# A decoder layer's expert loop: one copy of the down projection behind two copies of gate_up

## The chip, the cores and the metric

The kernel runs on one core of one Trainium2 chip. The metric is the device time of one execution in microseconds (us), lower is better. A core has five engines, each with a sequencer that reads its own stream of instructions: TensorE (PE; weight loads are listed as PEld, the sequencer's own instructions as PEldq), VectorE (DVE), ScalarE (ACT), GpSimd (POOL) and SyncE (SP). Sixteen DMA engines move data, and also instructions, from HBM.

## What is computed

One layer of a decoder: a mixer (retention and stick-breaking attention), then a mixture of experts over 1024 tokens of width 1024, top 4 of 32 experts. What matters here is the expert part:

```python
    def expert_block(args):
        xb, e = args
        gu = xb @ w_gate_up[e] + b_gate_up[e]
        gate = jnp.minimum(gu[:, 0::2], SWIGLU_LIMIT)
        up = jnp.clip(gu[:, 1::2], -SWIGLU_LIMIT, SWIGLU_LIMIT)
        hidden = (up + 1.0) * gate * jax.nn.sigmoid(SWIGLU_ALPHA * gate)
        return hidden @ w_down[e] + b_down[e]
```

The tokens of each expert are gathered, run through this block, weighed with their softmax share and added into the output. The number of tokens of an expert is known only on the chip.

## The kernel before

One block serves one expert with up to 168 tokens (CAP): 128 (P) in the main part and two overflow quarters of 32 (OV) behind them. An expert with more tokens would get further blocks behind the 32 (the second loop, L1165 to L1168). All engines run the blocks in step, tied by semaphores; every engine's order is written out by hand, no planner sets it. The weights of gate_up come in four DMAs of 2 MB and those of down in two, each issued by SP as soon as the block before has used its buffer.

PE's part of a block is block_matmuls (L1111 to L1145). In order: gate_up, for f in 0 to 7 (L1113): 16 fp32 products each (L1119) into bank 0 or 1, with a moving width of `w` tokens; token_list (24 small products for the next block's token list, L1053) behind f = 3; down's bias and its first half (t = 0, L1084 and L1099), each k waiting for the hidden rows that ACT and DVE made (h_lo) and for split weights (c_lo); the second half (t = 1) up to k = 3; turn_tokens, which transposes the next block's tokens (L1060, L1064); k = 4 to 6; the overflow rows' bias (L1090); the overflow rounds, down_over(0) if the block has over 128 tokens and down_over(1) if over 160 (L1107, 32 fp32 products each); and k = 7. An fp32 product of L1119 or L1107 is two MATMULs and two LDWEIGHTS in PE's stream.

The width must be fixed in the code, so there are two copies, WIDTHS = (140, 168). block_pe (L1147) loads the number of tokens into a register and choose (L1150) branches between them: the narrow copy for up to 140 tokens, the wide one for more. Each copy is all of block_matmuls, and the loop over the 32 experts (`with e.Fori(0, NE) as n`, L1163) holds both. In the built program PE's part of this loop is 1,838 instructions; the second loop has as many again. A narrow block runs the header and the narrow copy, then jumps (L1155) over the wide copy to the loop's end, and from there (L1163) back to the top. A wide block jumps over the narrow copy first.

Of the kernel before, what the change touches and what calls it, by code (L numbers as in the profile page):

```python
# [37 lines left out]
P = 128  # L38
# [12 lines left out]
OV = 32  # L51
# [66 lines left out]
def layer(nc, x, attn_norm_g, w_in, ret_norm_g, sb_q_norm_g, sb_k_norm_g, w_out, ffn_norm_g,  # L118
          w_router, b_router, w_gate_up, b_gate_up, w_down, b_down, consts, rope, out):
    with ExitStack() as ctx:  # L120
# [709 lines left out]
        def _(e):  # L830
# [210 lines left out]
            for j in range(NT - 1):  # L1041
                n = NT - 1 - j
# [7 lines left out]
            def token_list():  # L1050
                for h in range(NH):
                    for i in range(NT):
                        mm = e.matmul(bank[7][:, 5 * h:5 * h + 5], hot[:, i, h * P:(h + 1) * P], tw_s[:, i, :],  # L1053
                                      start=i == 0, stop=i == NT - 1)
                mm.then_inc(l_sum, 1)

            def turn_tokens():
                for m in range(2):
                    for q in range(4):
                        mm = e.transpose(bank[4 + m][:, q * P:(q + 1) * P], xg[:, (4 * m + q) * P:(4 * m + q + 1) * P], ident)  # L1060
                    mm.then_inc(g_tr, 1)
                for r in range(RO):
                    for c in range(2):
                        mm = e.transpose(bank[6][:, (2 * r + c) * P:(2 * r + c + 1) * P], xg_o[:, r, c * P:(c + 1) * P], ident)  # L1064
                    mm.then_inc(g_tr, 1)
# [17 lines left out]
            def down_bias(t):  # L1083
                e.matmul(bank[2 + t][:, :], sel, bias_d[:, t * CH:(t + 1) * CH], start=True, stop=False,  # L1084
                         skip_group_check=True)

            def over_bias():
                for r in range(RO):
                    for j in range(GR):
                        e.matmul(bank[7][quarter_rows(j), r * 2 * P:(r + 1) * 2 * P], sel[:, 0:OV],  # L1090
                                 bias_d[:, j * 2 * P:(j + 1) * 2 * P], start=r == 0, stop=False, skip_group_check=True)

            def down_main(n, t, k):
                if t == 0:
                    e.wait_ge(h_lo, n * 8 + (k + 1))
                if k % 2 == 0:
                    e.wait_ge(c_lo, n * 8 + (4 * t + k // 2 + 1))
                for h, w in ((hid_hi, dn_hi), (hid_lo, dn_hi), (hid_hi, dn_lo)):
                    mm = e.matmul(bank[2 + t][:, :], h[:, k], w[:, t, k], start=False, stop=k == KD - 1 and w is dn_lo,  # L1099
                                  skip_group_check=True)  # L1100
                if k == KD - 1:
                    mm.then_inc(m_dn, 1)

            def down_over(r):
                for k in range(KD):
                    for j in range(GR):
                        e.matmul(bank[7][quarter_rows(j), r * 2 * P:(r + 1) * 2 * P],  # L1107
                                 hid[:, k, P + r * OV:P + (r + 1) * OV], dn_ring[:, k, j * 2 * P:(j + 1) * 2 * P],
                                 start=False, stop=k == KD - 1, skip_group_check=True)

            def block_matmuls(n, w, tokens):  # L1111
                e.wait_ge(g_xT, n * 4 + 4)
                for f in range(KD):  # L1113
                    if f % 2 == 0:
                        e.wait_ge(gu_in[f // 2], n * 16 + 16)
                    e.wait_ge(m_up, n * 8 + (f + 1))
                    for part in range(2):
                        for k in range(KD):
                            mm = e.matmul(bank[f % 2][:, part * CAP:part * CAP + w],  # L1119
                                          gu_ring[:, k, f * 256 + part:(f + 1) * 256:2], xT[:, k, 0:w],  # L1120
                                          start=k == 0, stop=k == KD - 1)
                    mm.then_inc(m_gu, 1)
                    if f == 3:
                        e.wait_ge(l_hot, n + 2)
                        e.wait_ge(m_yo, n * 4 + 4)
                        token_list()
                e.wait_ge(s_sel, n + 1)
                down_bias(0)
                for k in range(KD):
                    down_main(n, 0, k)  # L1130
                down_bias(1)
                for k in range(4):
                    down_main(n, 1, k)
                e.wait_ge(g_in, n * 48 + 96)
                turn_tokens()
                for k in range(4, KD - 1):
                    down_main(n, 1, k)
                e.wait_ge(l_ok, n + 2)
                over_bias()
                with e.If(tokens > P):  # L1140
                    down_over(0)
                if w > P + OV:
                    with e.If(tokens > P + OV):
                        down_over(1)
                down_main(n, 1, KD - 1)  # L1145

            def block_pe(n):  # L1147
                tokens = e.value_load(it_i[0:1, 1, bass.ds(n, 1)], min_val=-S, max_val=S)

                def choose(widths):  # L1150
                    if len(widths) == 1:
                        block_matmuls(n, widths[0], tokens)
                        return
                    half = len(widths) // 2
                    with e.If(tokens <= widths[half - 1]):  # L1155
                        choose(widths[:half])
                    with e.Else():
                        choose(widths[half:])

                choose(WIDTHS)  # L1160

            e.wait_ge(it_step, 1)
            with e.Fori(0, NE) as n:  # L1163
                block_pe(n)
            more = e.value_load(it_i[0:1, 1, NI - 1:NI], min_val=0, max_val=NX - 1)  # L1165
            with e.If(more > 0):
                with e.Fori(NE, more + NE) as n:
                    block_pe(n)  # L1168
# [458 lines left out]
```

## Time and profile before

| | us |
|---|---|
| median of 3 runs | 2245.34 |
| lowest, highest | 2244.52, 2245.95 |
| the profiled execution | 2247.83 |
| its span, first to last instruction | 2246.0 |
| PE busy in it | 2148.1 (96%) |
| DVE busy | 1282.2 (57%) |
| ACT busy | 765.2 (34%) |

The profiled execution is 2.49 us above the median of the runs; 1.83 us of it lie outside the span. The mixer takes the first 650 us or so, the expert loop runs from about 670 us to 2229 us. A chain of waits is read from the last instruction backwards: at each step it names the work that the next one waited for. "issue" in it is time in which the engine waited for nothing that the profile shows. [...]

### The profile page before, as it was taken

To read this page: it belongs to the slowest core of one execution; us is meant where nothing else is said; L and a number is where in the kernel's file an instruction comes from. 1 tells how busy PE (TensorE), PEld (TensorE's weight loads), DVE (VectorE), ACT (ScalarE), POOL (GpSimd) and SP (SyncE) were. 2 spreads that over 40 slices of the span, in tenths; PEclk is the share of its full clock that TensorE was granted. 3 is DMA by queue.
4 is the path that set the end of the run, shared out by engine and by line. 5 is a ranking of instruction groups with operands and counts; after the bars stand their busy time and mean duration, and the time that the engine had idled before them with its cause. 6 is when DMAs were issued, how large, how long until landed. Compare 5 with 4: busy or idle time off the path is not lost.

```text
span 2246.0 us, 41668 instructions
## 1 busy us (share of the span) xinstructions
PE 2148.1 (96%) x16349; PEld 1929.3 (86%) x16350; DVE 1282.2 (57%) x2579; ACT 765.2 (34%) x1360; POOL 330.6 (15%) x237
## 2 busy tenths in 40 slices
PE   6999999899969999999999999999999999999996
PEld 5888888677858999899989998999899998999996
DVE  6434534786356565456656654665566665566654
ACT  3243133576113333233333332332333333333332
POOL 1100200200000211112112111111121211212111
PEclk9999999999969999999999999999999999999998
DMA  5231221304365888678979887887798897899983
GB/s 171 79 103 57 94 94 38 113 2 151 113 213 182 287 303 309 221 247 312 324 256 314 310 296 251 289 303 254 268 315 310 309 311 255 283 313 334 331 275 95
DMA packets 257670, 510.12 MB, mean 227 GB/s; under 512 B 7450, under 2 KB 44366, under 8 KB 257294
## 3 DMA queue, kind: packets, MB, share of 16 engines
q1 hardware_dynamic: 234268, 451.96, 56.7%
q0 software_dynamic: 21968, 51.67, 9.4%
q10 hardware_dynamic: 1344, 5.14, 0.7%
q8 instruction: 75, 1.23, 0.2%
q14 instruction: 15, 0.12, 0.0%
HBM read 473.09 MB, written 33.55 MB: 226 GB/s over the span
## 4 chain that ended last, share of the span: by engine, by line
PE 93%; issue 2%; DVE 2%; DMA 1%; POOL 0%; ACT 0%; SPq 0%; ACTq 0%; DVEq 0%; POOLq 0%
PE bank L1119 45%; PE bank L1099 16%; PE bank L860 13%; PE bank L1107 3%; PE bank L958 2%; PE bank L971 2%; PE bank L1005 1%; PE bank L1006 1%; PE bank L1007 1%; PE bank L1060 1%; PE bank L1053 1%; PE bank L942 1%; PE bank L1026 1%; PE bank L1064 1%; PE bank L1084 1%
## 5 line engine op out<-in xcount | busy, mean ns | idle before, releaser
L1119 PE MATMUL bank<-hx,ring 128*128 128x140 f32 (+1 forms) x8192 | 1035.3, 289 | 21.2 <-issue 18.8
L1119 PEld LDWEIGHTS bank<-hx,ring 128*128 128x128 f32 x8192 | 1027.4, 198 | 26.0 <-issue 21.0
L1099 PE MATMUL bank<-work_r,hx_r 128*128 128x512 f32 x1024 | 335.2, 408 | 0.0
L1551 DVE TENSOR_TENSOR mix_r<-ring,work_r 128x1024 fp32r<-128x1024 f32 x256 | 305.1, 1223 | 41.1 <-ACT work_r L792 41.0
L809 ACT ACTIVATE hx<-hx 128x168 f32<-128x168 f32 x256 | 87.9, 344 | 616.1 <-DVE hx L1567 615.0
L1567 DVE TENSOR_SCALAR hx<-bank,small 128x168 f32<-128x168 f32 x256 | 100.4, 392 | 307.7 <-PE bank L1119 307.5
L792 ACT ACTIVATE work_r<-ring 128x1024 fp32r<-128x1024 f32 x256 | 257.7, 1042 | 0.0
L1099 PEld LDWEIGHTS bank<-work_r,hx_r 128*128 128x128 f32 x1024 | 188.2, 189 | 43.8 <-issue 10.4
L1099 PE MATMUL bank<-mix_r,hx_r 128*128 128x512 f32 x512 | 200.0, 391 | 0.0
L800 ACT ACTIVATE hx<-bank,small 128x512 f32<-128x512 f32 x64 | 44.0, 688 | 314.6 <-PE bank L1064 167.9
L603 POOL DMA_INDIRECT out_x<-hx,small x32 | 51.9, 1622 | 658.6 <-ACT hx L802 639.6
L579 POOL DMA_INDIRECT hx<-xn_scratch,small x33 | 33.3, 1009 | 618.7 <-DVE small L1469 618.7
L860 PE MATMUL bank<-hx_r,mix_r 128*128 128x512 f32 x480 | 114.1, 396 | 7.6 <-DVE hx_r L1201 7.6
L815 ACT ACTIVATE hx_r<-hx 128x128 fp32r<-128x128 f32 x256 | 79.0, 308 | 109.7 <-DVE hx L1577 109.7
L860 PEld LDWEIGHTS bank<-hx_r,mix_r 128*128 128x128 f32 x480 | 90.7, 190 | 27.8 <-issue 9.1
L1099 PEld LDWEIGHTS bank<-mix_r,hx_r 128*128 128x128 f32 x512 | 96.1, 188 | 21.0
L860 PE MATMUL bank<-hx_r,work_r 128*128 128x512 f32 x480 | 113.7, 394 | 0.0
L1460 DVE TENSOR_TENSOR work<-hx,cst 128x3072 bf16<-128x3072 f32 x33 | 110.6, 3352 | 0.0
L860 PEld LDWEIGHTS bank<-hx_r,work_r 128*128 128x128 f32 x480 | 89.7, 188 | 20.2 <-issue 1.9
L606 POOL DMA_INDIRECT out_x<-hx,small x64 | 100.4, 1570 | 19.5 <-issue 19.5
L1569 DVE TENSOR_SCALAR hx<-bank,small 128x168 f32<-128x168 f32 x256 | 98.2, 384 | 0.0
L1474 DVE TENSOR_TENSOR hx<-bank,small 128x512 f32<-128x512 f32 x66 | 42.6, 686 | 85.9 <-PE bank L1060 85.9
(220 smaller groups left out, 2335.6 us busy)
## 6 DMA issues: line engine op xcount, KB each, us to landing
ring<-in_w_gate_up SPq DMA_DIRECT2D x128, 2048.0 KB, 12.7
ring<-in_w_down SPq DMA_DIRECT2D x64, 2048.0 KB, 13.8
mix<-in_w_in SPq DMA_DIRECT2D x14, 1024.0 KB, 5.1
work<-in_w_in SPq DMA_DIRECT2D x14, 1024.0 KB, 5.1
ring<-in_x SPq DMA_DIRECT2D x8, 512.0 KB, 8.9
hx<-in_w_out SPq DMA_DIRECT2D x1, 4096.0 KB, 14.7
work<-in_x ACTq DMA_DIRECT2D x8, 512.0 KB, 4.7
out_x<-work SPq DMA_DIRECT2D x8, 512.0 KB, 4.4
```

The lines of the kernel that those rows point to most:

```text
L606: e.indirect_dma_start(out=out_quarters, in_=y_o[:, r], in_offset=None, compute_op=ALU.add, out_offset=bass.IndirectOffsetOnAxis(ap=idx_sc ...
L792: e.activation(dn_hi[:, nh, k:k + 2], dn_ring[:, k:k + 2, nh * CH:(nh + 1) * CH], ACT.Copy).then_inc(c_hi, 1)
L809: e.activation(sg[:, f % 2], g1[:, f % 2], ACT.Sigmoid, scale=GALPHA).then_inc(m_sig, 1)
L815: e.activation(hid_hi[:, f], hid[:, f, 0:P], ACT.Copy).then_inc(h_hi, 1)
L860: mm = e.matmul(dst, lhs, rhs, start=k == 0 and (xs is x_hi and ws is w_hi), stop=k == KD - 1 and ws is w_lo)
L1099: mm = e.matmul(bank[2 + t][:, :], h[:, k], w[:, t, k], start=False, stop=k == KD - 1 and w is dn_lo, skip_group_check=True)
L1107: e.matmul(bank[7][quarter_rows(j), r * 2 * P:(r + 1) * 2 * P], hid[:, k, P + r * OV:P + (r + 1) * OV], dn_ring[:, k, j * 2 * P:(j + 1) * ...
L1119: mm = e.matmul(bank[f % 2][:, part * CAP:part * CAP + w], gu_ring[:, k, f * 256 + part:(f + 1) * 256:2], xT[:, k, 0:w], start=k == 0, sto ...
L1460: e.tensor_tensor(hot, pos_s.unsqueeze(2).to_broadcast([P, NT, NH * P]), slot_at.unsqueeze(1).to_broadcast([P, NT, NH * P]), ALU.is_equal) ...
L1551: e.tensor_tensor(dn_lo[:, nh, k:k + 2], dn_ring[:, k:k + 2, nh * CH:(nh + 1) * CH], dn_hi[:, nh, k:k + 2].bitcast(F32), ALU.subtract).the ...
L1567: e.tensor_scalar(g1[:, b], bank[b][:, 0:CAP], be[:, f:f + 1], GLIM, ALU.add, ALU.min)\
L1569: e.tensor_scalar(u1[:, b], bank[b][:, CAP:2 * CAP], be[:, 8 + f:9 + f], GLIM + 1.0, ALU.add, ALU.min).then_inc(m_up, 1)
```

## The change

block_matmuls is cut in two: gate_up(n, w), which still exists in two widths inside the choice, and down(n, tokens), which stands once behind it. With the second overflow round no longer tied to the wide copy, its test stands inside that of the first.

```diff
-            def block_matmuls(n, w, tokens):
+            def gate_up(n, w):
                 e.wait_ge(g_xT, n * 4 + 4)
                 for f in range(KD):
...
                         token_list()
+
+            def down(n, tokens):
                 e.wait_ge(s_sel, n + 1)
                 down_bias(0)
                 for k in range(KD):
...
                 over_bias()
                 with e.If(tokens > P):
                     down_over(0)
-                if w > P + OV:
                     with e.If(tokens > P + OV):
                         down_over(1)
                 down_main(n, 1, KD - 1)
...
                 def choose(widths):
                     if len(widths) == 1:
-                        block_matmuls(n, widths[0], tokens)
+                        gate_up(n, widths[0])
                         return
...
                 choose(WIDTHS)
+                down(n, tokens)
```

In the built program PE's part of the loop is now 1,569 instructions, again with a second loop like it. The products that a block executes are the same. On PE, at the end of the narrow gate_up, there stood before (each row is an instruction or a run of equal ones; ISA and REGISTER_ALU are the sequencer's register work, names in brackets are semaphores waited for):

```order
L1119 MATMUL bank1<-hx,ring 128x140 x15
L1127 REGISTER_ALU
L1084 MATMUL bank2<-cst,small 128x512 [waits s_sel]
L1099 MATMUL bank2<-work_r,hx_r 128x512 [waits c_lo,h_lo]
L1099 MATMUL bank2<-work_r,hx_r 128x512
```

and now:

```order
L1119 MATMUL bank1<-hx,ring 128x140 x15
L1156 UNCONDITIONAL_BRANCH
...
L1119 MATMUL bank1<-hx,ring 128x168 x15
L1158 UNCONDITIONAL_BRANCH
L1129 REGISTER_ALU
L1084 MATMUL bank2<-cst,small 128x512 [waits s_sel]
L1095 ISA
L1099 MATMUL bank2<-work_r,hx_r 128x512 [waits c_lo,h_lo]
L1099 MATMUL bank2<-work_r,hx_r 128x512
```

A narrow block now jumps (L1156) over the wide gate_up, and a register operation (L1095) stands ahead of each k of down's first half, where the numbers to wait for were kept from gate_up before. L1158 is a jump to the next instruction and isn't in the final stream.

On PE, at the overflow rounds and the end of the loop, there stood before in the wide copy:

```order
L1140 COMPARE_AND_BRANCH
L1107 MATMUL bank7<-ring,hx 32x256 x32
L1140 UNCONDITIONAL_BRANCH
L1143 COMPARE_AND_BRANCH
L1107 MATMUL bank7<-ring,hx 32x256 x32
L1143 UNCONDITIONAL_BRANCH
L1099 MATMUL bank3<-work_r,hx_r 128x512 x2
L1099 MATMUL bank3<-mix_r,hx_r 128x512
L1157 UNCONDITIONAL_BRANCH
L1163 REGISTER_ALU
L1163 COMPARE_AND_BRANCH
```

and now, for both widths:

```order
L1142 COMPARE_AND_BRANCH
L1107 MATMUL bank7<-ring,hx 32x256 x32
L1144 COMPARE_AND_BRANCH
L1107 MATMUL bank7<-ring,hx 32x256 x32
L1144 UNCONDITIONAL_BRANCH
L1099 MATMUL bank3<-work_r,hx_r 128x512 x2
L1099 MATMUL bank3<-mix_r,hx_r 128x512
L1165 REGISTER_ALU
L1165 COMPARE_AND_BRANCH
```

The narrow copy's exit (L1155 before) is gone, and a block with at most 128 tokens jumps over both rounds at once. L1165 is now what L1163 was, the jump back to the loop's top.

## Rows read from the trace of the kernel before

**Rows 1.** The page, chain that ended last by engine.

```profile
PE 93%; issue 2%; DVE 2%; DMA 1%; POOL 0%; ACT 0%; SPq 0%; ACTq 0%; DVEq 0%; POOLq 0%
```

**Rows 2.** PE groups by shape: line, tiles, shapes, count | busy us, mean ns | idle.

```profile
L1119 PE MATMUL bank<-hx,ring 128*128 128x140 f32 x6912 | 847.8, 285 | 18.0 <-issue 15.7 <-DVE hx L1569 1.5 <-DVE hx L1482 0.8
...
L1119 PE MATMUL bank<-hx,ring 128*128 128x168 f32 x1280 | 187.5, 309 | 3.1 <-issue 3.1
```

**Rows 3.** Chain in order of time (start us, us, what): undisturbed halves of gate_up.

```profile
870.94 18.24 PE bank L1119 x128
...
988.48 15.25 PE bank L1119 x128
...
2003.40 15.25 PE bank L1119 x128
...
2047.85 15.26 PE bank L1119 x128
```

**Rows 4.** The same chain: gate_up's end in block 1, and five gaps.

```profile
708.91 0.22 PE bank L1084
...
725.64 3.00 issue
728.64 17.19 PE bank L1119 x128
...
928.31 3.12 issue
931.43 21.39 PE bank L1119 x128
...
1370.89 4.31 issue
1375.20 18.38 PE bank L1119 x128
...
1572.53 4.13 issue
1576.66 18.34 PE bank L1119 x128
...
1907.27 4.29 issue
1911.56 18.15 PE bank L1119 x128
```

**Rows 5.** Stretches: us, busy us (count) of PE, PEld, DVE, ACT, POOL; clock, DMA, GB/s.

```profile
0.00:640.00 640.00, 600.21 (x3841) 502.51 (x3842) 333.53 (x456) 254.43 (x427) 57.55 (x39) 0.99 0.28 92
...
683.58:685.06 1.48, 0.00 (x1) 0.00 (x1) 1.02 (x4) 1.33 (x2) 0.00 (x0) 1.00 0.12 18
...
1375.20:1381.10 5.90, 5.90 (x25) 5.90 (x26) 0.00 (x0) 0.00 (x0) 3.06 (x2) 0.50 1.04 300
```

**Rows 6.** PE's sequencer by line: count, ns min/median/max, first and last start us.

```profile
L1127 PEldq ALU_OP  x1: 32/32/32, 706.6 to 706.6; - x1
...
L1155 PEldq COMPARE_BRANCH  x1: 3547/3547/3547, 723.3 to 723.3; - x1
...
L1163 PEldq COMPARE_BRANCH  x32: 67/209/4897, 727.0 to 2226.5; - x32
```

**Rows 7.** DMA queues (packets, MB, share): 0-640, 660-668, 870-925, 987-1036, 1036-1317 us (last two rows).

```profile
q8 instruction: 31, 0.51, 0.3%
...
q8 instruction: 1, 0.02, 0.9%
...
q8 instruction: 4, 0.07, 0.5%
...
q8 instruction: 3, 0.05, 0.4%
...
q1 hardware_dynamic: 37440, 75.50, 75.0%
q0 software_dynamic: 4032, 9.44, 13.7%
```

## The prediction

> **What bounds the kernel now.** First the page's chain of work that ended last: TensorE (PE) holds 93% of it, "issue" (PE waits for nothing that the profile shows) 2%, DMA 1% [rows 1]. So only what makes PE do less, or wait less, moves the end. The change removes no matmul, so the question is where PE stands still in the expert loop. The grouped PE instructions by shape give the blocks: 6912 of width 140 and 1280 of width 168, at 256 records a block, so 27 narrow and 5 wide, 32 in all, and no further block behind the 32 experts [rows 2]. The chain in order of time shows undisturbed blocks: the first half of gate_up (f 0 to 3) takes 15.25 or 15.26 us in a narrow one, 18.24 in a wide one, and narrow blocks without an overflow round follow each other every 44.45 us, 2003.40 to 2047.85, with no gap [rows 3]. The reader then looks for the pieces called "issue" between two blocks. There are five, of 3.00, 3.12, 4.31, 4.13 and 4.29 us, and behind each the first half of gate_up is about 3 us too long [rows 4]. The first stands behind the very first block, the other four each behind a wide one.
>
> Two views say what they are. The sequencer's branches: the jump back (L1163) takes 209 ns as a median but up to 4897, and the narrow copy's exit (L1155) took 3547 ns once, at 723.3 us [rows 6]; these are the branches just ahead of the gaps. The DMA queues by window: queue q8 carries only instructions, 16 KB a packet (0.51 MB in 31), and has a packet at just those jumps, while in the 281 us of six narrow blocks in a row it has none [rows 7]. So PE waits for its own code. [...]
>
> **What PE's code store holds.** I count code in the built programs and take its behaviour from the fetches. Up to 640 us, straight-line code, 31 fetches came [rows 7]; PE executed 3841 matmuls and 3842 weight loads there [rows 5], with waits about 256 instructions a fetch. Call that a page. The loop body is 1,838 PE instructions before and about 1,568 after: 7.2 and 6.1 pages. The 32nd fetch falls in 660 to 668 us [rows 7], when PE turned the biases (L1072), so a page begins 27 to 66 instructions ahead of the loop. The body thus touches pages 1 to 8 before, 1 to 7 after, with room of more than 100 instructions to either side.
>
> The fetches of the first wide block fit one rule: on entering a page the next is fetched if it doesn't already stand behind it, and eight are held. In 870 to 925 us there are four fetches [rows 7], pages 6, 7, 8 and, on entering page 8, the ninth. The ninth pushes out page 1, so the jump back misses: the gap of 3.12 us at 928.31 [rows 4]. The wide block after it needs pages 1, 4 to 8 and the ones ahead, 2 and 9: eight, and it ends without a gap: the next block starts at 988.48 and its first half takes 15.25 us [rows 3]. The narrow block then refetches three (987 to 1036) ahead of need, and narrow blocks alone (pages 1 to 4, 8, 9) need nothing. Each later wide block repeats it.
>
> [...]
>
> **The change part by part.**
>
> (1) The body shrinks. A wide block now runs 1, then 3 to 7, and the page fetched ahead at the end is the eighth. With eight held, nothing is pushed out. The four gaps behind wide blocks go. Each is worth its gap and the slow stretch, against 18.24 us for an undisturbed wide half and 15.26 for a narrow one [rows 3, 4]: 3.12 + (21.39 - 18.24) = 6.27; 4.31 + (18.38 - 15.26) = 7.43; 4.13 + (18.34 - 15.26) = 7.21; 4.29 + (18.15 - 15.26) = 7.18. Sum 28.1 us. All of it is on PE and on the path. Next late would be weights or DVE's results, but narrow blocks already follow each other at 44.45 us, the shortest period there is, with no wait [rows 3], so nothing stands behind the gap.
>
> (2) The first block. Before, its exit jump missed page 8: 3.00 + (17.19 - 15.26) = 4.93 us. That goes. In its place the jump from the narrow gate_up (page 3) to down (page 5) misses, as only page 4 was fetched ahead. The sequencer reaches that place at 706.6 us [rows 6], while PE goes from gate_up to down at 708.91 [rows 4], so 2.3 us of the 3.5 us are hidden by queued matmuls; with some 0.3 us of register work the gap is 1.5 us. Behind a 1.48 us gap the clock stayed up [rows 5]. Gain 3.4 us. Bounds: a 4.9 us branch makes the gap 2.9, and 3.1 us of slow clock may follow, a loss of 1.1; wholly hidden, a gain of 4.9.
>
> (3) Added to every narrow block: one taken jump over the wide gate_up (some 0.2 us: the median of L1163) and 9 register operations in down at 32 ns [rows 6], so 0.5 us on the sequencer. The exit jump of before falls away. Cover: the sequencer is 2.3 us ahead at the end of gate_up, and from there the pace of the queue, not of the sequencer, rules. Price on PE: 0. If the cover were gone: 0.2 us x 27 = 5 us.
>
> (4) Overflow rounds. A block of 129 to 140 tokens tests once more inside the first round; it saves the exit jump behind the last three matmuls. Equal, 0. With at most 128 tokens both rounds are jumped over, to page 7, which is held. 0. A wide block loses nothing.
>
> (5) Nothing is moved among DMA, DVE, ACT or POOL; no wait is added. PE's waits stand in the same order.
>
> **Sum.** 28.1 + 3.4 = 31.5 us. The profiled execution took 2247.83 us (span 2246.0), so 2216.3 there. It stands 2.5 us over the median of the three runs, 2245.34; from the median, 2213.8.
>
> **Rivals.**
>
> A. As forecast, 2209 to 2219: the bounds of (2) give 2212.3 to 2218.3, and the sizes of the four gaps vary by about 1 us each.
>
> B. The pages stay but the cover of (3) fails, since the sequencer's lead is smaller somewhere than the 2.3 us of rows 4 and 6, for instance behind an overflow round. For: I have rows for the lead at one place alone. Against: the header of a block gets no longer, and the added jump stands at that one place. 5 us back: 2219.
>
> C. No change. The code doesn't fit as I count it, or the store is not eight pages and wide blocks still end in a miss; part (2) swaps one miss for another. Time 2245.3. Against: five of five misses and all pauses of q8 fit eight. [...]
>
> D. Slower: the jump over the wide gate_up misses in every narrow block, because the next place after page 4 is refilled each time round. 26 blocks x 1.5 us = 39 us, less 31.5: 2253, and with slow clock behind each gap (3.1 us more) up to 2333. It decides from 21 such misses (31.5 / 1.5). For: the path now skips a part of the code mid-block. Against: before, narrow blocks skip pages 5 to 7 and miss nothing.
>
> **How the numbers follow.** A 0.85, B 0.07, C 0.04, D 0.04. 0.2% (4.5 us) is about what a measurement of this kernel can tell from no change. A and B are both faster: 0.92; C is the same: 0.04; D slower: 0.04. The range holds A and B with the bounds of (2) and a few us for gaps that differ between executions: 2207 to 2223; C and D, 8 in 100, stay outside.
>
> **What would show it.** Right: no "issue" piece between blocks behind a wide block; all jump-backs under 0.3 us; q8 with no packet from the second block to the end of the loop; granted clock 1.00 throughout the loop; one branch of over 3 us at about 706 us (L1156) and a gap of 1 to 3 us ahead of the first block's down. Part (3) wrong: gaps of 0.1 to 0.2 us ahead of L1084 or L1119 in narrow blocks. Wrong as a whole: q8 packets in narrow blocks, or a branch of over 3 us behind a wide block.

## The result, and the profile after

The changed kernel takes 2221.68 us, median of 4 runs (2220.20 to 2222.74), against 2244.93 for the kernel before in 4 runs: ratio 0.9892, 95% interval 0.9878 to 0.9906, 23.3 us less. The forecast was 2213.8, range 2207 to 2223. The direction and the main mechanism held; the size was 7.9 us off, and the time lies 1.3 us inside the range's slow end. Every kernel in the experiments below but wide_first and after_again was executed once, so small differences are read from the traces and not from those times.

The profiled execution of after took 2220.2 us, span 2218.3. Its chain of work that ended last, in order of time (start us, us, what), in the first block, around the first wide blocks and at the last block:

```profile
691.97 15.37 PE bank L1119 x128
707.34 4.37 issue
711.71 0.61 PE bank L1084
712.32 7.68 PE bank L1099 x24
...
731.05 15.29 PE bank L1119 x128
...
871.45 18.24 PE bank L1119 x128
...
927.93 0.89 PE bank L1099 x3
928.82 18.24 PE bank L1119 x128
...
981.81 0.90 PE bank L1099 x3
982.72 15.26 PE bank L1119 x128
...
2157.00 15.26 PE bank L1119 x128
```

Of the five gaps of [rows 4] none stands behind a block any more: 927.93 + 0.89 is 928.82, and the wide block that starts there needs 18.24 us for its first half where it took 21.39. One gap is new, of 4.37 us, inside the first block, between gate_up and down, and the 24 products behind it take 7.68 us where 5.46 is usual.

The sequencer's branches of after (count, ns min/median/max): first the jump over the wide gate_up in the first block, then the jump back, which was 209 and up to 4897 ns [rows 6].

```profile
L1156 PEldq COMPARE_BRANCH  x1: 6506/6506/6506, 705.0 to 705.0; - x1
...
L1165 PEldq COMPARE_BRANCH  x32: 76/208/237, 729.2 to 2198.6; - x32
```

Stretches of after (start:end and length in us; busy us and count of PE, PEld, DVE, ACT, POOL; clock; DMA share; GB/s): the branch over the wide gate_up, the products behind it, and the loop from the second block to near its end:

```profile
705.05:711.56 6.51, 2.29 (x20) 2.09 (x18) 4.44 (x10) 3.35 (x7) 0.00 (x0) 0.89 1.02 348
712.00:716.90 4.90, 4.90 (x13) 3.84 (x13) 1.78 (x2) 0.15 (x1) 0.00 (x0) 0.50 0.66 247
735.00:2195.00 1460.00, 1460.00 (x11931) 1348.23 (x11930) 885.47 (x1978) 487.01 (x894) 257.72 (x186) 1.00 0.87 294
```

For 1460 us PE is busy without a break, at a granted clock of 1.00. (The granted clock is a share of PE's full speed.) The DMA queues of the same stretch (packets, MB, share) answer to [rows 7]: q8, which carries PE's code, is not among them.

```profile
q1 hardware_dynamic: 188899, 380.91, 72.9%
q0 software_dynamic: 20832, 48.77, 13.6%
q14 instruction: 1, 0.01, 0.0%
```

### The profile page after: what moved, and what is told of

It is laid out like the page before. It is cut to its first block, busy times and chain, and to the rows that moved or that the text cites. A ratio compares the mean times of both kernels' runs of the same rounds, so it can differ in the third digit from the quotient of the medians.

```text
span 2218.3 us, 41969 instructions
## 1 busy us (share of the span) xinstructions
PE 2134.1 (96%) x16349; PEld 1916.6 (86%) x16350; DVE 1282.0 (58%) x2579; ACT 765.1 (34%) x1360; POOL 330.6 (15%) x237
## 4 chain that ended last, share of the span: by engine, by line
PE 94%; DVE 2%; issue 2%; DMA 1%; ACT 0%; POOL 0%; ACTq 0%; SPq 0%; DVEq 0%; POOLq 0%
PE bank L1119 45%; PE bank L1099 16%; PE bank L860 13%; PE bank L1107 3%; PE bank L958 2%; PE bank L971 2%; PE bank L1060 1%; PE bank L1005 1%; PE bank L1007 1%; PE bank L1006 1%; PE bank L1053 1%; PE bank L942 1%; PE bank L1064 1%; PE bank L1084 1%; PE bank L1026 1%
## 5 line engine op out<-in xcount | busy, mean ns | idle before, releaser
L1119 PE MATMUL bank<-hx,ring 128*128 128x140 f32 (+1 forms) x8192 | 1021.8, 287 | 2.5 <-DVE hx L1571 1.7
L1119 PEld LDWEIGHTS bank<-hx,ring 128*128 128x128 f32 x8192 | 1014.7, 197 | 5.7 <-DVE hx L1571 1.9
L606 POOL DMA_INDIRECT out_x<-hx,small x64 | 100.4, 1569 | 19.5 <-issue 19.5
```

The lines of the kernel that those rows point to most:

```text
L606: e.indirect_dma_start(out=out_quarters, in_=y_o[:, r], in_offset=None, compute_op=ALU.add, out_offset=bass.IndirectOffsetOnAxis(ap=idx_sc ...
L1119: mm = e.matmul(bank[f % 2][:, part * CAP:part * CAP + w], gu_ring[:, k, f * 256 + part:(f + 1) * 256:2], xT[:, k, 0:w], start=k == 0, sto ...
```

## The experiments

The theory is the prediction's: eight pages held, the one fetched ahead among them, and a block that needs nine misses at the jump back. Its rivals: each jump or instruction costs a little; the single down matters; the length of the loop matters. A second question is why the first block's miss cost 5.5 us more than forecast.

**two_copies_short.** Both copies stay whole, but the wide one loses the code of its second overflow round, so that the loop ends in page 7. The kernel so leaves out some work: rows 161 to 168 of one expert get no down product, 3.5 us on PE.

```diff
-                if w > P + OV:
-                    with e.If(tokens > P + OV):
-                        down_over(1)
```

> The kernel before, with both copies whole, but without the code of the second overflow round (rows 161 to 168 of an expert get no down product; one expert here has them, 3.5 us of PE work). PE's loop is 1,706 instructions instead of 1,838, so with a start 27 to 66 instructions into a page it ends in page 7 instead of 8. Theory (what matters is how many pages the loop touches, eight held): no miss behind wide blocks, the four gaps and slow stretches of 28.1 us are gone though down still stands twice; one miss in the first block stays. Profiled span about 2246 - 28 - 3.5 = 2214 to 2219 us, q8 silent from the third block to the end of the loop. Rival (it takes the single down and the shorter jumps): gaps behind wide blocks stay, 2242 us.

Measured 2217.73 us, span 2215.9. Its chain around the wide blocks, and q8 from 740 to 2190 us:

```profile
925.17 0.89 PE bank L1099 x3
926.06 18.24 PE bank L1119 x128
...
979.08 0.89 PE bank L1099 x3
979.97 15.26 PE bank L1119 x128
```

```profile
q8 instruction: 3, 0.05, 0.0%
```

The gaps behind wide blocks are gone with down still standing twice and the exit jump and the jump back as before; the first block's stays, 2.84 us at 727.02. Some 130 instructions fewer did it. The single copy of down is not needed for the gain; a shorter loop is enough. Whether pages or instructions are what counts, the next pairs ask. The three packets on q8 all lie in 870 to 926 us, during the wide copy's first run, and fit its pages fetched ahead. The expectation of a silent q8 overlooked them. PE waits for nothing from 780 us to the end of the loop.

**pad_end_1, pad_end_2, pad_mid_2.** The changed kernel with code added that should never be executed, at the end of the loop or ahead of down:

```diff
                 down(n, tokens)
+                with e.If(tokens > S):
+                    for _ in range(2):
+                        down_over(0)
```

> The changed kernel with a never executed piece of code at the end of the loop (an overflow round under a condition that never holds), 128 matmul and load instructions plus a branch, which every block jumps over. The loop grows from 1,569 to some 1,700 instructions and still ends in page 7 (1,724 to 1,766 of 1,792). Theory (eight pages held, the loop's pages and the one ahead must fit): nothing changes, 2218 to 2224 us, q8 silent from the third block on. Rival (each instruction or jump more costs): the time grows with the code, 5 us or more.

> The same with two such rounds, 256 instructions: the loop ends in page 8, so each block enters page 8, the ninth is fetched ahead and page 1 is lost. Theory: every block, narrow too, misses at the jump back, and as the pages behind are then displaced in turn, narrow blocks miss again at the jump to down. 31 jumps back at 6.3 to 7.4 us make +195 to +230 us; with the second miss at 3 to 6.8 us some +290 to +440 us: 2415 to 2660 us, and q8 moves some 6 to 9 packets a block. Rival (code size costs little by little, or the store has room for a ninth): within 10 us of pad_end_1.

> The same 256 never executed instructions, but between the choice and down. The loop is as long as in pad_end_2. Theory (what counts are the pages that a block touches, with the ones ahead, not the length of the loop): a narrow block touches 1 to 3 and 6 to 8 with 4 and 9 ahead, eight, so narrow blocks miss nothing; a wide block touches 1 to 9 and loses page 1: misses behind the wide blocks as in the kernel before, 4 of them at 6.3 to 7.4 us, plus up to 4 at the first jump to down behind them: 2247 to 2275 us. Rival (the length of the loop counts): as pad_end_2.

They took 2223.58, 2222.63 and 2222.71 us, with 40 packets on q8 in pad_end_2 as in after. This told nothing on the theory: tokens is declared to be at most S, so the compiler had dropped the added code, and the built streams hold two instructions more, or none. They count as three more executions of the changed kernel.

**code_end_1, code_end_2.** The same at the end of the loop, with a condition that the compiler can't decide.

```diff
                 down(n, tokens)
+                with e.If(tokens > 3 * P):
+                    for _ in range(2):          # code_end_1: range(1)
+                        down_over(0)
```

> The changed kernel with 130 instructions that are never executed at the end of the loop (one overflow round under the condition of more than 384 tokens, which no expert here has); every block jumps over them. The loop is 1,700 instructions and, from a start 27 to 66 into a page, still ends in page 7. (In pad_end_1, pad_end_2 and pad_mid_2 the compiler had dropped the added code as unreachable: their built loops had 1,570 instructions.) Theory (eight pages held): 2218 to 2224 us, q8 silent from the third block on. Rival (each instruction or jump more costs): 5 us or more longer.

> The same with 258 such instructions: the loop is 1,830 instructions and ends in page 8, so every block enters page 8, the ninth is fetched ahead and page 1 is lost. Theory: each block misses at the jump back, 31 times 6.3 to 7.4 us, and narrow blocks again at the jump to down, 3 to 6.8 us: +195 us at the least, +440 us at the most: 2415 to 2660 us, q8 moves 6 to 9 packets a block. Rival (the store has room for a ninth, or something other than pages made the misses behind wide blocks): within 5 us of code_end_1.

Measured 2223.56 us with one round and 2768.76 us with two. The jump back and the span, first of code_end_1, then of code_end_2:

```profile
span 2221.7 us, 42001 instructions
...
L1168 PEldq COMPARE_BRANCH  x32: 76/208/214, 731.8 to 2202.5; - x32
```

```profile
span 2766.8 us, 42001 instructions
...
L1168 PEldq COMPARE_BRANCH  x32: 76/7376/8148, 735.2 to 2749.9; - x32
...
L1156 PEldq COMPARE_BRANCH  x59: 79/6296/6987, 672.1 to 2732.6; - x59
L1163 PEldq COMPARE_BRANCH  x32: 442/3085/3538, 732.0 to 2746.8; - x32
...
PE bank L1119 <- issue: 303.9, 31, 17.3
PE bank L1084 <- issue: 114.8, 27, 4.7
```

By the traces, the 130 instructions cost 1.0 us: from the start of the third block to that of the last it is 778.15 to 2160.57, 1382.42 us, against 1381.42 in after. 128 more on top of these cost 545 us, though both kernels execute the same 42001 instructions and neither executes the added rounds. The step lies between a loop of 1,700 and one of some 1,829 instructions; by the prediction's count, with the loop starting 27 to 66 instructions into a page, page 7 ends at 1,726 to 1,765. So the rival of a small price for each instruction falls. The 545 us are idle time of 303.9 us ahead of gate_up and 114.8 us ahead of down (4.2 of these in code_end_1 too) and 130.1 us more of PE busy (2268.1 against 2138.0 us), at a mean clock of 0.898 against 0.982. It went past the expectation's top of 2660 us: most blocks missed not twice but three times, also at the jump over the added code into page 8 (L1163, 3.1 us as a median), and the pieces ahead of gate_up average 9.8 us, slow clock not counted, where 6.3 to 7.4 us with it had been expected.

**code_mid_2.** The same 258 instructions between the choice and down.

> The same 258 instructions between the choice and down. The loop is as long as in code_end_2. Theory (the pages that a block touches count, with those ahead): narrow blocks touch 1 to 3 and 6 to 8 with 4 and 9 ahead, eight, and miss nothing; wide blocks touch all and lose page 1: 4 misses behind wide blocks at 6.3 to 7.4 us, and up to 5 at the next jump to down: 2247 to 2280 us. Rival (the length of the loop counts): as code_end_2.

Measured 2781.94 us, near code_end_2. By what was written ahead that speaks for the rival, the loop's length. But the test of the condition stands in page 5 itself: a narrow block that jumps to it touches page 5 and needs nine pages after all. Its branches fit that, missed on the way to the test (L1156, median 6146 ns of 59) and again from the test to down:

```profile
L1162 PEldq COMPARE_BRANCH  x32: 356/5667/6212, 715.8 to 2745.0; - x32
```

The edit didn't separate the two readings, so it was made again:

**code_wide_2.** The same instructions at the end of the wide gate_up, test included, where only wide blocks come by.

```diff
                         gate_up(n, widths[0])
+                        if widths[0] == CAP:
+                            with e.If(tokens > 3 * P):
+                                for _ in range(2):
+                                    down_over(0)
                         return
```

> In code_mid_2 the test of the added condition stands itself in page 5, so a narrow block touched page 5 on its way and needed nine pages after all; that run did not tell the set of pages from the length of the loop. Here the same 258 never executed instructions, test included, stand at the end of the wide gate_up, so that a narrow block jumps from page 3 straight to down in page 6. The loop is 1,829 instructions as in code_end_2. Theory (the pages that blocks touch count, with those ahead, eight held): narrow blocks touch 1 to 3, 6 to 8 with 4 and 9 ahead, eight, and after a narrow block nothing is missed; wide blocks touch all nine and lose page 1: 5 misses at the jump back behind wide blocks at 6.3 to 7.4 us, and one or two at a wide block that follows one: 2255 to 2275 us, under 100 packets on q8. Rival (the length of the loop counts): as code_end_2, 2769 us and 320 packets.

Measured 2261.16 us, with 85 packets on q8. Its chain has five gaps behind the first block's, each behind a wide block:

```profile
930.23 9.47 issue
939.70 20.47 PE bank L1119 x128
...
995.84 4.43 issue
1000.27 17.90 PE bank L1119 x128
...
1385.30 4.31 issue
1389.61 17.80 PE bank L1119 x128
...
1586.35 4.57 issue
1590.92 17.83 PE bank L1119 x128
...
1921.00 4.38 issue
1925.38 17.86 PE bank L1119 x128
```

The loop is as long as in code_end_2 but for one instruction, and costs 508 us less. What counts is the set of pages that a block passes, with the ones fetched ahead. The first of these gaps is two misses in a row, back to page 1 (3.9 us, at 928.0) and on to the wide gate_up (6.6 us, at 932.8), since two wide blocks follow each other there.

**late_loads.** Why did the first block's miss take 6.5 us? SP here holds back the weights of expert 1 until the first gate_up is done.

```diff
-            with e.Fori(1, NE) as n:
+            e.wait_ge(m_gu, KD)
+            load_expert(1, 1)
+            with e.Fori(2, NE) as n:
                 load_expert(n, n)
```

> The changed kernel; SyncE holds back the gate_up weights of expert 1 until the first block's gate_up is done (about 707 us), so that fewer transfers are under way when the first block's jump misses. Theory (the code fetch waits for its turn among data transfers: branches that missed took 3.55 and 3.87 us at a DMA share of 0.02 and 0.01 over the branch, 4.7 to 4.9 us at 0.32 to 0.41, 6.51 us at 1.02): the branch takes 3.5 to 5 us, the gap ahead of down is 1.5 to 3 us. Rival (a jump to a page two further on, or that kind of branch, is slow by itself): 6.5 us and a gap of 4.4 us as before. The block behind may wait for its weights, which is not the point of this run.

Measured 2219.14 us. The branch, its gap with what follows, and two stretches of late_loads (lines stand two further on than in after):

```profile
L1158 PEldq COMPARE_BRANCH  x1: 3906/3906/3906, 707.6 to 707.6; - x1
...
709.92 1.77 issue
711.69 0.39 PE bank L1086
712.08 7.16 PE bank L1101 x24
...
707.63:711.54 3.91, 2.29 (x20) 2.09 (x18) 2.87 (x7) 0.79 (x3) 0.00 (x0) 1.00 0.21 50
713.00:716.40 3.40, 3.40 (x10) 2.63 (x9) 3.37 (x3) 1.73 (x2) 0.00 (x0) 0.50 1.05 403
```

3.91 us at a DMA share of 0.21, where the same jump took 6.35 us in after_again at a share of 1.03, 6.51 in after at 1.02 and 6.30 in code_end_1 at 1.00. The kind and the length of the jump are the same, so the rival falls: with fewer transfers under way the fetch is shorter. Misses in other places fit: 3.55 us at 0.02 and 4.90 at 0.33 in the kernel before. At a share of about 1 the price is not one number, though: a jump back took 7.44 us at 1.00 in code_end_2. The kernel with quiet queues was executed once, and what in the DMA engines makes the fetch wait was not tried. Here the second surprise shows as well: after a gap of only 1.77 us the clock fell to 0.50 for 3.4 us, some 1.3 us into the products, and the 24 products took 7.16 us instead of 5.46.

**wide_first and after_again.** A version that avoids the miss's price: the wide gate_up stands first, so that the first block misses in its header, while PE is ahead of VectorE's tables, and narrow blocks fall through into down.

```diff
-                    with e.If(tokens <= widths[half - 1]):
-                        choose(widths[:half])
-                    with e.Else():
+                    with e.If(tokens > widths[half - 1]):
                         choose(widths[half:])
+                    with e.Else():
+                        choose(widths[:half])
```

> The changed kernel with the wide gate_up ahead of the narrow one in the code: a narrow block now jumps over the wide gate_up in its header and then falls through into down; a wide block jumps over the narrow gate_up instead. Theory (the 5.5 us that the forecast was off in the loop are the first block's miss on the way to down: a branch of 6.51 us at 705.05, a gap of 4.37 us and some 2.3 us of slow clock): that miss moves to the header of the first block, where PE is ahead of VectorE's tables anyway (it waits 1.68 us for them at 681.8 us), so it costs 0.3 to 2.5 us in place of 6.8. Time 4 to 6.5 us below the changed kernel: 2215 to 2218 us. q8 stays silent from the third block on. Rival (the loss is not tied to that jump): within 1 us of the changed kernel's time.

> The changed kernel as it is, beside wide_first on the same chip, as its yardstick: 2221.7 us, with one branch of 5 to 7 us at about 705 us and no other above 1 us until the loop ends.

On one chip, in 4 runs each: wide_first 2214.71 us (ratio to before 0.9855, interval 0.9839 to 0.9872), after_again 2222.62 (0.9885, 0.9868 to 0.9901), before 2247.21 in 7. Wide_first is 7.9 us below the changed kernel; its slowest run (2216.12) lies below after_again's fastest (2218.80). Its branch and its first block in the chain:

```profile
L1156 PEldq COMPARE_BRANCH  x1: 3399/3399/3399, 670.9 to 670.9; - x1
...
673.14 1.50 issue
674.64 9.44 PE bank L1119 x64
...
684.85 7.90 PE bank L1119 x64
692.75 0.59 PE bank L1053 x24
693.34 15.37 PE bank L1119 x128
708.70 0.22 PE bank L1084
708.92 5.46 PE bank L1099 x24
```

The miss takes 3.4 us, at a DMA share of 0.02, and down follows gate_up without a gap. It holds PE up by 1.50 us at 673.14, and the 64 matmuls behind it take 9.44 us, yet it delays nothing: from turning the first tokens (L1060) to f = 2 it is 15.11 us, 669.74 to 684.85, as in after, 668.37 to 683.48. PE's f = 0 and 1 end at 684.08 and VectorE goes on at 684.10, so the cover is just used up; a longer miss there would cost time. The expectation of 4 to 6.5 us was low, as the miss cost nothing there. From f = 2 to the end of the loop wide_first takes 7.0 us less than after_again; the rest of the 7.9 lies ahead of that place, which two executions of the changed kernel reach at 683.48 and 686.07 us.

## Why the prediction was right, and where it was off

**The cause of the gaps.** Right. PE waited for its own code behind wide blocks, and eight pages with one ahead explain the kernel before, after, two_copies_short, both sides of the step in code_end_1 and code_end_2, and code_wide_2. The page's size is measured in the kernel before, at 255.7 instructions of PE a packet over the first 32 packets; that eight are held is the author's estimate from that size and the step between code_end_1 and code_end_2. The last section has the figures of both. Rival C (no change) falls with PE's 1460 us without a break, during which, by the count, each narrow block jumps from page 3 to 5 and from 7 to 1. None of them had to fetch: no packet comes on q8, and none of the 57 passes of L1156 between 720 and 2200 us takes over 209 ns, nor any jump back (L1165) over 237 ns.

**Part (1), 28.1 us.** Right to a tenth. From the start of the third block to that of the last it was 2184.66 - 775.07 = 1409.59 us before, and 2157.00 - 775.58 = 1381.42 after: 28.2 us less. The sizes come from the same execution of before that is compared here, so the close fit says that the four gaps went whole and nothing else moved, not that the gaps have these sizes in every execution. The slow stretch behind each of the four is one of clock: in before PE is granted 0.50 for 5.97 us from 931.43, 5.90 from 1375.20, 5.84 from 1576.66 and 5.44 from 1911.56.

**Part (2), the first block, gain 3.4 us.** This is the step that failed: the measured result is a loss of about 2.1 us, so even its sign was wrong. The third block starts at 775.58 instead of 775.07, though gate_up of the first ended 1.57 us earlier (707.34 against 708.91 in [rows 4]): 1.57 + 0.51 = 2.08. The bound of 1.1 us of loss was passed too. Two assumptions were wrong. The branch was priced at 3.5 us, from a miss at a DMA share of 0.02, and took 6.51 in the middle of the weight loads, with a gap of 4.37 us instead of 1.5. The cover was right: the branch began 2.29 us before PE ran out of products (705.05 and 707.34). And the clock was taken to stay up behind it, where it fell; the bias and the 24 products took 0.39 + 2.22 us longer. The row at 683.58 in [rows 5] shows the clock inside a gap; the stretch of before that follows it shows that it did stay up there:

```profile
685.06:692.00 6.94, 6.94 (x58) 6.94 (x59) 5.83 (x11) 0.98 (x4) 0.00 (x0) 1.00 0.81 300
```

But late_loads shows it fall behind 1.77 us, so one such row did not make a gap of 1.5 us a safe case. With that, 5.5 of the 7.9 us are placed.

**Parts (3) to (5), 0 us.** Right. PE has no wait in the loop from the second block on, so the jump over the wide gate_up, the register operations and the nested test are covered. Rival B falls.

**The rest.** The sum for the span is 28.2 - 2.1 = 26.1, and the spans differ by 27.7; the other 1.6 us lie ahead of the first block's f = 2, in work that the change doesn't touch, and differ from execution to execution (after_again reaches that place 2.6 us later than after). So the profiled execution of after, forecast at 2216.3, took 2220.2: 3.9 us off, which is 5.5 less 1.6. Against the medians another 4.0 come on top: the profiled execution of before stood 2.5 us above the median that the forecast used, and that of after 1.5 below its own. In after_again the medians differed by 24.6. That the time still fell into the range is partly luck: the bounds of (2) end at 2218.3, and only the few us added for executions that differ reach over 2221.7.

**Rival D (slower).** It did not come in this kernel, but code_end_2 shows the jump over the wide gate_up missing in every narrow block, there for want of a ninth page, and with the other misses at a far higher price than I gave it: 545 us. code_end_1 shows that 130 instructions more cost 1.0 us, and code_end_2 that 258 cost 545 more.

## What to carry to other kernels

If an engine's loop has branches and the profile shows "issue" gaps just behind a jump, look at that engine's branch times and at the instruction queue, and count the pages that an iteration passes, including the one fetched ahead. Here duplicated code cost next to nothing while the pages fitted; one page more, and every iteration that passed them all paid, so shared code matters for where the total ends. Where a first pass must miss, put the jump where the engine is ahead of the others and the DMA queues are quiet.

## What the runs showed of the hardware

- PE's code came in pages of about 256 instructions. In the kernel before, the 32nd packet on q8, of 16 KB like every other, starts at 664.50 us; the trace lists 8183 instructions of PE ahead of it (3921 matmuls, 3921 weight loads and 341 others, nearly all waits), 255.7 a packet. From the first packet, at 42.54 us behind 208 instructions, to the 32nd it is 7975 in 31 steps, 257.3 each.
- One page came ahead of need. In two_copies_short the first wide block has packets at 878.81, 894.46 and 910.58 us, 263 and 227 listed instructions apart, and PE waits for nothing from 860 to 1000 us. In after the missed jump at 705.05 us has a packet at 709.05 and, 29 listed instructions further on, a second at 714.87.
- Eight pages held fit all kernels here, by estimate from that size: a loop of 1,700 instructions (code_end_1: seven pages and the one ahead) had no packet on q8 from 740 to 2195 us, one of some 1,829 (code_end_2: eight and the one ahead) had 320 in all, and took 545 us longer.
- A missed branch took from 2.9 us at a DMA share of 0.02 (L1163 in code_end_2, at 793.4 us) to 8.1 us (its longest jump back). The same jump took 3.9 us at a share of 0.21 and 6.3 to 6.5 at 1.00 to 1.03.
- A gap of 1.77 us in PE's work was followed by 3.4 us at a granted clock of 0.50 in late_loads, where a gap of 1.48 us in the kernel before left it at 1.00. The two places differ in more than the gap, and no run separates that.
- A taken branch with its target held took some 0.2 us (L1165, median 208 ns), wholly hidden in the 1460 us where PE had queued work.
